# Latent attention in a two-block transformer kernel: the queries' rotation as a step of its own, its sine product on GpSimd, and other places for odd heads, last heads and gate tiles

## The reference

```python
q = (rmsnorm(c_q, q_a_g) @ w_q_b).reshape(b, s, 8, 192)      # c_q: 384 wide
q_nope = q[..., :128]
q_rope = rope(q[..., 128:], cos, sin)                        # x1*cos - x2*sin, x2*cos + x1*sin
kv = (rmsnorm(c_kv, kv_a_g) @ w_kv_b).reshape(b, s, 8, 256)  # c_kv: 256 wide
k_nope, v = kv[..., :128], kv[..., 128:]
sc = (q_nope @ k_nope^T + q_rope @ rope(k_rope)^T) * 192 ** -0.5
p = softmax(where(key <= query, sc, -1e30))                  # whole softmax per query
yb = (p @ v) * silu(gb)                                      # gb: the gate, 1024 wide
x = x + concatenate([ya, yb]) @ w_out
```

## Time and profile before

| | us |
|---|---|
| median of three runs | 2789.79 |
| profiled execution | 2790.87 |
| its span | 2789.1 |
| PE busy | 2732.7 (98% of the span) |
| PE weight loads | 2271.2 (81%) |
| DVE | 1241.8 (45%) |
| POOL | 1089.6 (39%) |
| ACT | 1000.0 (36%) |

### The profile page before, as it was taken

The page is one execution under the profiler, slowest core; times in us unless marked ns, Lnnn a source line. Parts: engine busy times, 40 slices in busy tenths (PEclk is TensorE's granted clock), DMA queues, the critical chain, the costliest instruction groups (busy, mean ns, idle before and its releaser), DMA issues.

```text
span 2789.1 us, 33326 instructions
## 1 busy us (share of the span) xinstructions
PE 2732.7 (98%) x13100; PEld 2271.2 (81%) x13100; DVE 1241.8 (45%) x1831; ACT 1000.0 (36%) x1566; POOL 1089.6 (39%) x544
## 2 busy tenths in 40 slices
PE   8999998999999999899999999999999999999997
PEld 7888887888888888788878888888878888888886
DVE  6466636622346663672335545553443222222223
ACT  5244435523223443553433333332223323332222
POOL 1443332344443433334443333334344444444442
PEclk9999999999999999999999999999999999999998
DMA  6432231254443223124442232222223333336333
GB/s 183 132 84 76 73 121 45 66 142 143 123 132 91 69 76 121 45 67 138 138 120 76 76 83 76 73 80 80 87 83 121 113 109 111 114 113 211 117 125 113
DMA packets 307611, 289.13 MB, mean 104 GB/s; under 512 B 33152, under 2 KB 256000, under 8 KB 306944
## 3 DMA queue, kind: packets, MB, share of 16 engines
q1 hardware_dynamic: 300512, 264.40, 32.0%
q10 hardware_dynamic: 6944, 22.61, 2.1%
HBM read 260.19 MB, written 26.74 MB: 103 GB/s over the span
## 4 chain that ended last, share of the span: by engine, by line
PE 84%; DVE 11%; DMA 2%; ACT 1%; issue 1%; POOL 0%; SPq 0%; DVEq 0%; ACTq 0%
PE bank L873 25%; PE bank L875 24%; PE bank L874 24%; PE work L1131 1%; DMA w_raw<-in_w_in 1%; DVE pt L1728 1%; PE o_bank L874 1%; PE o_bank L875 1%; DVE mixed L1475 1%; PE work L987 1%; PE work L989 1%; PE o_bank L873 1%; DMA latent_scr<-mixed 1%; DVE probs L1680 1%; DVE mixed L1471 1%
## 5 line engine op out<-in xcount | busy, mean ns | idle before, releaser
L850 POOL TENSOR_TENSOR w_lo<-w_raw,w_hi 128x1024 fp32r<-128x1024 f32 (+3 forms) x460 | 982.0, 2137 | 1367.5 <-ACT w_hi L699 1367.5
L873 PE MATMUL bank<-act_in,w_hi 128*128 128x512 f32 x2662 | 1054.0, 396 | 12.8 <-DVE act_in L1443 9.9
L875 PE MATMUL bank<-act_in,w_lo 128*128 128x512 f32 x2662 | 1041.0, 391 | 0.0
L874 PE MATMUL bank<-act_in,w_hi 128*128 128x512 f32 x2662 | 1039.7, 391 | 0.0
L699 ACT ACTIVATE w_hi<-w_raw 128x1024 fp32r<-128x1024 f32 (+3 forms) x468 | 438.0, 937 | 1049.3 <-PE bank L875 648.4
L873 PEld LDWEIGHTS bank<-act_in,w_hi 128*128 128x128 f32 x2662 | 501.0, 188 | 116.8 <-DVE act_in L1443 11.2
L875 PEld LDWEIGHTS bank<-act_in,w_lo 128*128 128x128 f32 x2662 | 500.5, 188 | 107.2
L874 PEld LDWEIGHTS bank<-act_in,w_hi 128*128 128x128 f32 x2662 | 501.2, 188 | 98.9 <-issue 1.7
L873 PE MATMUL bank<-mixed,w_hi 128*128 128x512 f32 x768 | 299.7, 390 | 0.0
L875 PE MATMUL bank<-mixed,w_lo 128*128 128x512 f32 x768 | 299.1, 389 | 0.0
L874 PE MATMUL bank<-mixed,w_hi 128*128 128x512 f32 x768 | 299.0, 389 | 0.0
(11 more groups left out here) (267 smaller groups left out, 2703.7 us busy)
## 6 DMA issues: line engine op xcount, KB each, us to landing
w_raw<-in_w_in SPq DMA_DIRECT2D x512, 128.0 KB, 2.5
w_raw<-in_w_in SPq DMA_DIRECT2D x224, 256.0 KB, 2.9
w_raw<-in_w_out SPq DMA_DIRECT2D x64, 512.0 KB, 3.7
w_raw<-in_w_in SPq DMA_DIRECT2D x32, 512.0 KB, 3.7
w_raw<-in_w_out SPq DMA_DIRECT2D x64, 256.0 KB, 4.6
x_scr<-buf ACTq DMA_DIRECT2D x32, 256.0 KB, 3.2
probs<-x_scr SPq DMA_DIRECT2D x32, 256.0 KB, 5.0
w_raw<-in_w_attn_up SPq DMA_DIRECT2D x32, 256.0 KB, 2.9
```

What stands on the lines that cost most here:

```text
L850: nc.gpsimd.tensor_tensor(lo, raw, hi, ALU.subtract).then_inc(lo_ready, 1)
L873: pe.matmul(dst, lhs[0], rhs[0], start=start, stop=False, skip_group_check=skip)
L874: pe.matmul(dst, lhs[0], rhs[1], start=False, stop=False, skip_group_check=skip)
L875: return pe.matmul(dst, lhs[1], rhs[0], start=False, stop=stop, skip_group_check=skip)
```

## The change

- In `mla0` tile 0 is now `qr both` and tile 1 `qn`; the banks stay.
- Tile 0's `read` is only DVE's cosine product, straight after the product, before ACT's copies: ACT waits for it and then makes the four swapped copies. POOL multiplies the swapped copy by sin in place.
- A new step `rotate` (two slots after tile 0's product, four in the first pair) holds the sum, the casts and the low halves on DVE. Even heads' scores wait for it through a new semaphore; tile 4, which now shares its bank with tile 0's copies, waits for ACT.
- Odd heads 1, 3, 5: scores and normalising at 3 slots instead of 4, transposes at 6 instead of 7. The last pair's transposes, values and output come one slot later.
- Gate tiles: (log, min, mul) at 1, 4, 6; 16, 19, 21; 24, 27, 29; 32, 35, 37 slots after the gate's product instead of 4, 7, 9; 11, 13, 15; 22, 28, 30; 32, 38, 40.

```diff
-            group("mla0", l, h // 2, [], ["qn", "qr both", "kn", "v both, half the tokens", "v, other half"],
+            group("mla0", l, h // 2, [], ["qr both", "qn", "kn", "v both, half the tokens", "v, other half"],
...
+                if kind == "mla0" and m == 0:
+                    later(4 if i == 0 else 2, "rotate", n)
+            lag = {3: 3, 4: 2}.get(m) if kind == "mla0" else None
-            lag = {1: 1, 3: 3, 4: 2}.get(m) if kind == "mla0" else None
...
-            head("mla", l, 2 * i, 0, [(1, "mla_scores"), (1, "mla_norm"), (4, "transpose"), (7, "values"),
-                                      (10, "output")])
+            head("mla", l, 2 * i, 0, [(1, "mla_scores"), (1, "mla_norm"), (4 if i < 3 else 5, "transpose"),
+                                      (7 if i < 3 else 8, "values"), (10, "output")])
...
-            head("mla", l, 2 * i + 1, 0, [(4, "mla_scores"), (4, "mla_norm"), (7, "transpose"),
-                                          (8 if i < 3 else 10, "values"), (12, "output")])
+            head("mla", l, 2 * i + 1, 0, [(3 if i < 3 else 4, "mla_scores"), (3 if i < 3 else 4, "mla_norm"),
+                                          (6 if i < 3 else 8, "transpose"), (8 if i < 3 else 11, "values"),
+                                          (12 if i < 3 else 13, "output")])
...
-                    at = ((4, 7, 9), (11, 13, 15), (22, 28, 30), (32, 38, 40))[k]
+                    at = ((1, 4, 6), (16, 19, 21), (24, 27, 29), (32, 35, 37))[k]
...
# ACT, step "hi"
-                    if g["kind"] == "mla0" and m == 1:
+                    if g["kind"] == "mla0" and m == 0:
+                        act.wait_ge(bank_free, tile_no[gi, m] + 1)
...
# POOL
+                elif name == "hi" and groups[step[1]]["kind"] == "mla0" and step[2] == 0:
+                    g = groups[step[1]]
+                    swapped = probs2[:, T:2 * T]
+                    pool.wait_ge(mla_hi, swaps_before(step[1]) + 1)
+                    nc.gpsimd.tensor_tensor(swapped, swapped, sin[:, :], ALU.mult).then_inc(sin_done, 1)
...
# PE, product and mla_scores of even heads
+                if first and kind == "mla0" and m == 4:
+                    pe.wait_ge(mla_hi, swaps_before(gi) + 1)
+                        pe.wait_ge(queries_rotated, rotated_before(group_at["mla0", h["l"], h["h"] // 2]) + 1)
...
# DVE, read_mla
+                if g["kind"] == "mla0" and m == 0:
+                    full(gi, m)
+                    v.tensor_tensor(probs2[:, 0:T], src[:, :], cos[:, :], ALU.mult).then_inc(bank_free, 1)
...
+            def rotate_queries(gi):
+                c, swapped = probs2[:, 0:T], probs2[:, T:2 * T]
+                v.wait_ge(sin_done, rotated_before(gi) + 1)
+                link(v.tensor_tensor(c, c, swapped, ALU.add))
+                for e in range(2):
+                    ins = v.tensor_copy(qr_mla(e)[ROPE * e:ROPE * e + ROPE, :], c[ROPE * e:ROPE * e + ROPE, :])
+                link(ins)
+                for e in range(2):
...
+                    ins = v.tensor_tensor(qr_mla(e)[other, :], c[own, :], qr_mla(e)[own, :].bitcast(F32),
+                                          ALU.subtract)
+                ins.then_inc(queries_rotated, 1)
```

More of the change, by code:

```diff
@@ L387, in mla_dst @@
             if m < 3:
-                return (qn_mla(0), None, kn_mla(0))[m]
+                return (None, qn_mla(0), kn_mla(0))[m]
             return v_mla(g["i"])[:, :, 2 * (m - 3):2 * (m - 3) + 2, :].rearrange("p s b c -> p s (b c)")
@@ L423, in gate_views, with swaps_before, rotated_before @@
             return [(gate[:, :, :], tmp[:, :, :])]
+        def swaps_before(gi):
+            return 28 * groups[gi]["l"] + 7 * groups[gi]["i"]
+        def rotated_before(gi):
+            return 4 * groups[gi]["l"] + groups[gi]["i"]
         def mix_gate(k):
@@ L443, in hybrid_program @@
         pv_done = sem("pv_done")
+        sin_done = sem("sin_done")
+        queries_rotated = sem("queries_rotated")
         y_done = sem("y_done")
@@ L959, in product @@
                     if kind in ("mla0", "mla1"):
-                        cols = (128, 256) if kind == "mla0" and m == 1 else (0, 128)
+                        cols = (128, 256) if kind == "mla0" and m == 0 else (0, 128)
                         x = latent(kt if what == "q_b" else 3 + kt)
@@ L1425, in read_mla @@
                 his[0] += 1
[L1426 to L1430, removed]
+                if g["kind"] == "mla0" and m == 0:
+                    full(gi, m)
+                    v.tensor_tensor(probs2[:, 0:T], src[:, :], cos[:, :], ALU.mult).then_inc(bank_free, 1)
                     v.wait_ge(bank_free, tile_no[gi, m] + 1)
[L1432 to L1441, removed]
                 else:
+                    v.wait_ge(mla_hi, his[0])
                     v.tensor_tensor(dst[:, 1], src[:, :], dst[:, 0].bitcast(F32), ALU.subtract).then_inc(bank_free, 1)
@@ L1445, in read_mla @@
                 signal(tile_ready)
+            def rotate_queries(gi):
[6 more added lines that the diff above has]
+                for e in range(2):
+                    own, other = slice(ROPE * e, ROPE * e + ROPE), slice(ROPE * (1 - e), ROPE * (1 - e) + ROPE)
+                    ins = v.tensor_tensor(qr_mla(e)[other, :], c[own, :], qr_mla(e)[own, :].bitcast(F32),
+                                          ALU.subtract)
+                ins.then_inc(queries_rotated, 1)
             def read(gi, m):
@@ L1543, in _ @@
                     read(*step[1:])
+                elif name == "rotate":
+                    rotate_queries(step[1])
                 elif name == "q_split":
```

## The result

The changed kernel takes 2817.35 us (median of four runs, 2816.18 to 2821.05), the kernel before, run beside it, 2789.76: ratio 1.0097, interval 1.0079 to 1.0114. It is slower by 27.6 us where I forecast 13; 2817 lies above the range of 2788 to 2812. The profiled execution has a span of 2815.3.

The account below looks back on a forecast made before the run. PE bounds the kernel, with 11.1 us of waits on DVE in layer 0's latent attention. Layer terms +6.1 and +6.85, together +13.0 on 2790.87, gave 2803.8, less 1.1 for the median: 2803 us, range 2788 to 2812.

Parts of the forecast that it names:

- B0: Layer 0, start of h0's scores (B even heads, A odd): 436.8 for 436.69, the wait split in two, not shortened.
- B0 to A1: First pair, h0's scores to h1's: query product now behind the scores, h1 at 449.2 for 451.75, 1.85 us won.
- A1 to B1: Odd half, h1's scores to h2's: rotation behind the normalising, 15.2 us, each odd half 0.25 to 0.45 slower.
- B1 to A2: Even half with gate tile 1, h2's scores to h3's: 15.0, or 1.7 more if POOL is first; 15.8 taken.
- A2 to B2: Odd half, h3's scores to h4's: 15.2 us, with PE waiting 1.8 at the bank.
- B2 to A3: Even half with gate tile 2, h4's scores to h5's: gate product 1.9 for 0.7 beside POOL, 14.2 us.
- A3 to B3: Odd half with gate tile 3, h5's scores to h6's: ACT waits for DVE's step until 14.3; 17.2 us.
- the clock's term of the sum: First pair's scores, wait 2.7 instead of 4.0, clock may be back up: 0.75 us gain in layer 0, none in layer 1.
- The rival: The clock falls again behind PE's waits, 2.25 us each, twice per layer, +9: 2812 us; chance 0.20.
- The toss-up: Pair 1, gate product and POOL's 1.83 low half start within 0.1 us; POOL first costs 1.7 more, half taken.
- Gate tiles hold nobody: Rival: ACT's queue has other room; only the first pair's gain and three odd halves count, 2788 us; chance 0.22.
- Faster: Rival: PE's waits were DVE's load; key low half in time for bank 2, 7.4 us less per layer, 2775; chance 0.10.

Follow-up runs that it names:

- the second kernel of the experiments: The kernel before with only the gate tiles at their new slots, all else as before; 2812.14 us, ratio 1.0066.

## Why the prediction was wrong

By its own steps, for layer 0. Each is the time from one start of scores to the next; forecast, measured, and what the difference is.

| step | forecast | measured | difference |
|---|---|---|---|
| B0 (h0), before's zero | 436.8 | 437.86 | +1.06: POOL |
| B0 to A1 | 12.4 | 13.90 | +1.50: clock |
| A1 to B1 | 15.2 | 15.05 | -0.15 |
| B1 to A2 | 15.8 | 16.64 | +0.84: POOL |
| A2 to B2 | 15.2 | 17.83 | +2.63: clock |
| B2 to A3 | 14.2 | 14.36 | +0.16 |
| A3 to B3 | 17.2 | 18.52 | +1.32: clock |

The differences add to 7.4 us, twice that to 14.7, and the result was 14.35 above the forecast: the whole miss is in this table. The steps marked "clock" start with scores that ran 1.55, 2.75 and 1.57 us longer than at full clock. In the changed kernel with its waits filled the same three steps take 12.32, 15.69 and 17.56 us in layer 0, near the forecast's 12.4, 15.2 and 17.2.

- *The clock failed, three quarters of the miss* (5.45 of 7.36). The step is the clock's term of the sum: a gain of 0.75 us in layer 0, and nothing for any other wait in either layer. Instead PE's busy time rose by 9.2 us. The rival had 0.20 and a price of 4.5 per layer. PE fell back three times per layer: at the waits of 2.50 and 3.68 us, at that of 4.13, and at that of 1.81 ahead of h5. The scores took 5.43, 6.63 and 5.45 for 3.88: 1.55, 2.75 and 1.57. My own steps held the warning. Pair 1 was to stall 2.7 or 4.4 us, and the one fall in the trace of before stood behind 4.00. In pair 0 I wrote of waits of 2.7 and about 1, but with PE going on at 432.66 and 1.36 of product the scores at 436.8 mean a second wait of 2.8. "No wait of up to 1.1 us did" said nothing of those between 1.1 and 4. There the length alone doesn't decide: 1.98 us ahead of h6 was followed by 3.88 of scores, 1.81 ahead of h5 by 5.45, and 1.53 in the second kernel of the experiments by 5.46; 1.83 ahead of h5 in the kernel with the sine back on DVE was followed by 3.88. The rule cited for that rival (the Trainium skill, TensorE: Matmul & The Clock Gate, "HAM oscillation — how this bites in real kernels": bursts after idling start at the lower clock) was the better forecast; the trace agrees with it at three waits per layer, and not at those of 1.50 and 1.98 us, behind which PE ran at full clock.
- *The toss-up was no toss-up.* I gave half a chance to POOL's low half being ahead of the gate product in pair 1. It was ahead by 0.06 us in layer 0 and the product took 2.29; layer 1 has the same step to within a tenth. The forecast's other branch was 1.7 more than the first and half of that is the +0.84; and the branch that came true is also the one with the 4 us wait, behind which the clock fell. The second kernel of the experiments has the same hold (2.30 us, POOL 0.06 ahead) with the rotation untouched. The mean of two branches was the price of neither.
- *B0.* I had the gate product held by POOL until 433.65, and it was not (0.69 at 432.11). Held were the sum (1.00 at 432.95, for 0.69), beside POOL's 432.60, and the rotation's first low half (the two took 2.33 for 1.39), behind POOL's 434.48. So the forecast had the hold once, where it came twice.
- *Right:* the direction; the 15.2 of an odd half; DVE idle 2.2 us ahead of the odd reciprocal; the waits of 1.5 (forecast 1.8) at bank 2; waits ahead of h3 and h6 that end on the probabilities' low halves; none ahead of h1's transposes. Two of the six steps between scores hit within 0.2 us. The sine ran beside DVE's reading of PSUM in the first pair, as I had said (427.83 to 429.12, beside a low half at 428.41 of the usual 0.69).
- *A slip without effect on the sum.* For the odd half before I wrote 14.5; 14.06 and 14.25 with 0.7 on top are 14.8 and 14.95, from which the 0.25 to 0.45 do follow. The sign "odd halves under 14.5" was thus set too low; measured was 15.05, so it decides nothing.
- *The rivals that fell.* "Gate tiles hold nobody" would have given even halves of 12.3; moved apart they do give 12.36 (in that kernel h2 461.30 to h3 473.66, h4 488.75 to h5 501.11). "Faster" would have needed the rotation to end early: putting it between the maxima and the normalising did that, and brought 10 us of it, but at the change's gate places it ends above before; only the kernels with the gate tiles apart end under it.

Open stays how the 19.0 us of waits split between gate tiles and rotation, since the single edits do not add, and what makes one wait of 1.5 to 2 us cost the clock and another not, even at one place of one kernel. One such fall is 1.5 us and more, so a single trace of a kernel can mislead by that. The gate tiles apart changed the gaps within a tile and the slots together, so what the gaps alone bring is not shown. Nor was a kernel tried in which POOL's hold is gone: the one-operand product did not take it away.

## What to carry to other kernels

A stall of the matmul engine has two prices, its length and the lower clock behind it, and the second belongs in the sum for every wait longer than those after which the trace still shows full speed. A step of three engines (a low-priority one such as a gate's) is better spread so that none of its parts is issued just behind the one that it waits for; here that, with other slots for the parts, was worth 30 us, more than the change had cost. Where a step is put in the order decides as much as on which engine it runs: put work into the idle time of the engine that other work is waited for, and not behind it, and look for the next wait that takes its place.

## What the runs showed of the hardware

- More work made the kernel faster: 24 us of matmuls that nobody reads, in PE's waits, took 7.2 us off, as the granted clock kept 0.97 and 0.99 for 0.95.
- The same wait at the same place does not always cost the clock: in the kernel with the gate tiles apart, h0's scores took 3.85 us in layer 0 and 5.44 in layer 1, behind 2.00 and 2.01 us.
- A DVE operation on SBUF that starts just behind a POOL operation was held to its end and some tenths beyond, with two SBUF operands (2.29 us for 0.69) and with one (2.03 for 0.43). One that reads PSUM was not, in the one place looked at, in the kernel with rotation and gate tiles both moved; DVE, then POOL:

```profile
498.56 1.52 DVE L1454 TENSOR_TENSOR act_in<-bank,act_in 128x512 fp32r<-128x512 f32 x2
```

```profile
498.87 1.84 POOL L864 TENSOR_TENSOR w_lo<-w_raw,w_hi 128x768 fp32r<-128x768 f32 x1 [0.52 <-ACT w_hi L712]
```

The last 1.2 us of the two low halves lie beside POOL's 1.84 us, and they are no longer than two of 0.69 with the gap of 0.15 between them (1.53).
